# The first three levels of the next head's inverse move into the PE groups of this head's last three

## What is computed

```python
kk = jnp.einsum('bhcid,bhcjd->bhcij', kc, kc)
tri = jnp.where(strict, bc[..., :, None] * kk * decay, 0.0) + jnp.eye(CHUNK, dtype=f32)
rhs = jnp.concatenate([vc * bc[..., None], kc * (bc * jnp.exp(G))[..., None]], axis=-1)
sol = lax.linalg.triangular_solve(tri, rhs, left_side=True, lower=True, unit_diagonal=True)
u, w = sol[..., :GDN_DV], sol[..., GDN_DV:]
...
def step(S, inp):
    v_new = u_c - w_c @ S
    o = qd_c @ S + qk_c @ v_new
    S = cd_c * S + kd_c.T @ v_new
    return S, o
o = rmsnorm(o, o_norm_g) * silu(gate)
```

## Time and profile before

| | before |
|---|---|
| median of the runs | 1357.52 us |
| the profiled execution's own time | 1352.9 us |
| its span, first to last instruction | 1351.1 us |
| PE busy | 98% of the span |
| VectorE busy | 58% |
| ScalarE busy | 44% |
| granted PE clock, mean | 0.998 of full speed |

### The profile page before, as it was taken

How to read it: one execution, slowest core, us unless ns; L and a number is a source line. 1 busy time by engine, 2 the same in 40 slices (tenths; PEclk the granted TensorE clock), 3 DMA queues, 4 the chain that set the end, 5 groups by cost and what they waited for, 6 DMA issues and landing times.

```text
span 1351.1 us, 21851 instructions
## 1 busy us (share of the span) xinstructions
PE 1322.4 (98%) x8305; PEld 1061.6 (79%) x8305; DVE 779.4 (58%) x1160; ACT 600.5 (44%) x940; POOL 0.2 (0%) x4
## 2 busy tenths in 40 slices
PE   7899999999999999999999999999999999999998
PEld 5677777776888888888887877778888888888886
DVE  6787888887464344343455677776543433434555
ACT  5565556655353133231345667754431422313342
POOL 0000000000000000000000000000000000000000
PEclk9999999999999999999999999999999999999999
DMA  4332222321333323333333322224333333333323
GB/s 157 95 79 41 70 77 62 78 62 48 114 105 99 104 83 105 93 102 100 85 102 126 109 63 63 63 79 156 94 109 94 94 96 91 109 93 93 93 82 105
DMA packets 42342, 124.02 MB, mean 92 GB/s; under 512 B 3952, under 2 KB 12720, under 8 KB 41776
## 3 DMA queue, kind: packets, MB, share of 16 engines
q1 hardware_dynamic: 33472, 116.95, 28.8%
q10 hardware_dynamic: 8816, 6.33, 2.6%
HBM read 119.04 MB, written 4.23 MB: 91 GB/s over the span
## 4 chain that ended last, share of the span: by engine, by line
PE 88%; DVE 5%; ACT 4%; issue 2%; DMA 1%; ACTq 0%; DVEq 0%; SPq 0%
PE acc L333 26%; PE acc L335 25%; PE acc L334 25%; DVE wl L309 1%; DVE work L1716 1%; PE ps L485 1%; ACT wh L302 1%; PE ps L455 1%; PE ps L705 1%; PE ps L428 1%; DMA work<-rows 1%; PE ps L678 1%; PE ps L333 1%; PE ps L335 0%; PE ps L334 0%
## 5 line engine op out<-in xcount | busy, mean ns | idle before, releaser
L333 PE MATMUL acc<-xh,wh 128*128 128x512 f32 x1008 | 414.4, 411 | 11.5 <-DVE xl L1899 8.2
L335 PE MATMUL acc<-xh,wl 128*128 128x512 f32 x1008 | 394.8, 392 | 0.0
L334 PE MATMUL acc<-xl,wh 128*128 128x512 f32 x1008 | 394.3, 391 | 0.0
L302 ACT ACTIVATE wh<-raw 128x1024 fp32r<-128x1024 f32 x207 | 216.9, 1050 | 183.5 <-DMA raw<-in_weights 165.6
L309 DVE TENSOR_TENSOR wl<-raw,wh 128x1024 fp32r<-128x1024 f32 x207 | 253.0, 1222 | 67.5 <-ACT wh L302 64.6
L333 PE MATMUL acc<-yh,wh 128*128 128x512 f32 x608 | 238.1, 392 | 0.0
L334 PE MATMUL acc<-yl,wh 128*128 128x512 f32 x608 | 236.6, 389 | 0.0
L335 PE MATMUL acc<-yh,wl 128*128 128x512 f32 x608 | 236.6, 389 | 0.0
L333 PEld LDWEIGHTS acc<-xh,wh 128*128 128x128 f32 x1008 | 190.0, 188 | 52.6 <-DVE wl L309 10.1
L335 PEld LDWEIGHTS acc<-xh,wl 128*128 128x128 f32 x1008 | 189.9, 188 | 41.0
L334 PEld LDWEIGHTS acc<-xl,wh 128*128 128x128 f32 x1008 | 190.4, 189 | 36.0 <-issue 2.6
(11 more groups left out here) (252 smaller groups left out, 1105.8 us busy)
## 6 DMA issues: line engine op xcount, KB each, us to landing
raw<-in_weights SPq DMA_DIRECT2D x208, 512.0 KB, 3.5
work<-rows ACTq DMA_DIRECT2D x16, 256.0 KB, 7.1
h<-in_xT SPq DMA_DIRECT2D x4, 512.0 KB, 6.0
proj<-work ACTq DMA_DIRECT2D x2, 1024.0 KB, 5.3
work<-proj SPq DMA_DIRECT2D x2, 1024.0 KB, 6.7
outT<-h SPq DMA_DIRECT2D x8, 256.0 KB, 2.4
cst<-in_cst SPq DMA_DIRECT2D x1, 512.0 KB, 3.1
work<-in_pT SPq DMA_DIRECT2D x1, 512.0 KB, 4.6
```

The costliest lines, as they stand in the source:

```text
L302: nc.scalar.activation(slot(u)[0][:], raw[u.const % 2][:], ACT.Copy).then_inc(hi_done, 1)
L333: nc.tensor.matmul(dst[:], hi, mh[:, k, :], start=(n == 0), stop=False)
L334: nc.tensor.matmul(dst[:], hi, ml[:, k, :], start=False, stop=False)
L335: mm = nc.tensor.matmul(dst[:], lo, mh[:, k, :], start=False, stop=(n == KT - 1))
```

## The change

Two heads are now in work at once. The inverse's levels 1 to 3 of head i ("early") are computed in the same PE groups as levels 4 to 6 of head i-1 ("late"), so that a head has 6 groups (`x_group`, `tx_group`, r = 0, 1, 2). In a group the late matmuls come first, then 16 early ones on 32x32 tiles into another bank or another part of the bank. The level-6 matmuls are now 8 on tiles of 64 rows by 32 columns. Head 0's early levels stand alone, in six groups, and the last head's late levels too.

The early inverse lives as packed 32-wide blocks (128x128 instead of 128x512), so VectorE's masks, additions and transposes shrink to 64 or 128 columns, and after level 3 the blocks are put back on the diagonal of `TT` by four small transposes. `k`, `Lt`, `Ti`, the decay table, exp(G) and k by token have two buffers, and GpSimd copies `k` and `Lt` from the early buffer to the late one, 128x512 each, once per head. Because levels are ahead, the unit order changes to k of head i+1, then q, v and gate of head i; PE begins with five units, and period 7 has three. ScalarE copies k by token out of PSUM first (`act_ksq`) and scales it later (`token_k`). The ones matmul of the norm becomes two matmuls on a high and a low part (`osh` by ScalarE, `osl` by VectorE). The qk step moves from os(0) to v(3). On PE periods 2 to 6 are a loop and period 7 is written out; on VectorE and ScalarE all periods are written out, with no loop.

The diff, cut to its core:

```diff
+        kcs, qc, vc, sq, dbeta = [W(0), W(14)], W(1), W(2), W(3), W(4)
+        T64, xrstd = W(5)[:, 0:C * HD], W(6)
+        Tis = [W(5)[:, 2 * P:3 * P], W(5)[:, 3 * P:]]
...
-        TT0, xrstd = W(5), W(6)
-        Ti, TT, Xs, kb, kd, vb = W(16), W(17), W(18), W(19), W(20), W(21)
...
+        Tts, TT0, Xe = [W(16)[:, 0:P], W(16)[:, P:2 * P]], W(16)[:, 2 * P:3 * P], W(16)[:, 3 * P:3 * P + HD]
+        TT, Xl, kb, kd, vb = W(17), W(18)[:, 0:C * HD], W(19), W(20), W(21)
...
+        def kk_bank(j):
+            return ps[4 if isinstance(j, int) and j == 1 else 0]
...
+        def pe_norm(pe, j):
+            pe.wait_ge(ones_d, 1)
+            pe.wait_ge(s_d, j * 3 + 3)
+            pe.wait_ge(osh_d, j + 1)
+            nc.tensor.matmul(ps[4][:], ones_r, osh, start=True, stop=False)
+            pe.wait_ge(osl_d, j + 1)
+            nc.tensor.matmul(ps[4][:], ones_r, osl, start=False, stop=True).then_inc(oss_d, 1)
...
+        def x_group(pe, i, r, late, early):
+            b, e = i - 1, i
+            if late:
+                if r == 0:
+                    pe.wait_ge(te_d, b * 4 + 4)
+                    if not isinstance(i, int) or b > 0:
+                        pe.wait_ge(l_kept, b)
+                else:
+                    pe.wait_ge(tl_d, b * 2 + r)
+                if r == 2:
+                    pe.wait_ge(t64_d, b + 1)
+            if early:
+                pe.wait_ge(te_d, e * 4 + r + 1)
+                pe.wait_ge(ktok_d, 2 if isinstance(e, int) and e == 0 and r > 0 else e + 1)
+            small_tile(pe, i)
+            if late:
+                Lt, Ti = Lts[0], Tis[0]
+                for c in range(C):
+                    if r == 0:
+                        for lo in range(0, P, 32):
+                            q = slice(lo, lo + 32)
+                            last = nc.tensor.matmul(blk32(ps[0], c)[q], ch(Lt, c)[q, q], blk32(Ti, c)[q],
+                                                    start=True, stop=True)
+                    elif r == 1:
+                        for lo in (0, HD):
+                            one, two = slice(lo, lo + 32), slice(lo + 32, lo + HD)
+                            last = nc.tensor.matmul(blk32(ps[0], c)[two], ch(Lt, c)[one, two], blk32(Ti, c)[one],
+                                                    start=True, stop=True)
+                    else:
+                        for lo in (HD, HD + 32):
+                            q = slice(lo, lo + 32)
+                            last = nc.tensor.matmul(ps[0][q, c * HD:(c + 1) * HD], ch(Lt, c)[0:HD, q],
+                                                    T64[0:HD, c * HD:(c + 1) * HD], start=True, stop=True)
+            if early:
+                Lt, Ti = Lts[now(e)], Tis[now(e)]
+                for c in range(C):
+                    for lo in range(0, P, 32):
+                        q = slice(lo, lo + 32)
+                        last = nc.tensor.matmul(blk32(ps[2], c)[q], ch(Lt, c)[q, q], blk32(Ti, c)[q],
+                                                start=True, stop=True)
+            last.then_inc(xg_d, 1)
...
+            if early:
+                Tt = Tts[now(e)]
+                for c in range(C):
+                    to = slice(c * 16, (c + 1) * 16)
+                    for lo in range(0, P, 32):
+                        q = slice(lo, lo + 32)
+                        last = nc.tensor.matmul(ps[1][:, 2 * P:][q, to], blk32(TT0 if r == 0 else Tt, c)[q], Xe[q, to],
+                                                start=True, stop=True)
+            last.then_inc(txg_d, 1)
...
-                pe.wait_ge(tt_d, i * 6)
+                pe.wait_ge(ttl_d, i * 3)
+                if early:
+                    pe.wait_ge(te_d, i * 4 + 4)
+                pe.wait_ge(kbkd_d, i)
                 for c in range(1, C):
...
-        FILL = [0, 2, 2, 0, 2, 2, 2, 2, 2, 2, 2, 2, 2, 1, 1, 1, 1, 1, 1, 1, 1, 1, 1]
-        FIRST_FILL = [6, 2, 2, 0, 1, 2, 1, 2, 1, 2, 1, 2, 1, 1, 1, 1, 1, 1, 1, 1, 1, 1, 0]
-        assert sum(FILL) == sum(FIRST_FILL) == 4 * KT
...
+        def pe_first_steps(pe):
+            def x(r):
+                return lambda: x_group(pe, 0, r, False, True)
+            def tx(r):
+                def step():
+                    tx_group(pe, 0, r, False, True)
+                    if r == 0:
+                        pe_ktr(pe, 1)
+                        pe_kk(pe, 1)
+                return step
+            return [x(0), tx(0), x(1), tx(1), x(2), tx(2)]
...
+        FILL = [3, 3, 0, 3, 3, 3, 3, 2, 1, 2, 1, 2, 1, 2, 1, 2]
+        FIRST_FILL = [2, 1, 1, 1, 1, 1, 1] + [2, 2, 0, 1, 2, 1, 2, 1, 2, 1, 2, 1, 2, 1, 2, 2]
+        SHORT_FILL = [2, 2, 0, 2, 2, 2, 2, 2, 1, 2, 1, 1, 1, 1, 1, 2]
+        LAST_FILL = [1, 2, 0, 1, 2, 1, 2, 1, 1, 1, 2, 1, 2, 1, 2, 5, 10]
         OUT_AHEAD = ((5,), (5,), (5,), (5,), (), (), (), (2,))
-        LAST_FILL = [1, 1, 0, 1, 1, 1, 1, 1, 1, 2, 2, 1, 1, 1, 1, 1, 1, 1, 1, 1, 1, 3, 10]
-        assert sum(LAST_FILL) == 5 * (KT - 1)
+        assert sum(FILL) == sum(FIRST_FILL) == 4 * KT and sum(SHORT_FILL) == 3 * KT and sum(LAST_FILL) == 5 * (KT - 1)
...
+            gates = dict(zip((8, 12, 17, 21), pe_gate_steps(pe)))
+            for n in range(5 * KT):
+                if n in gates:
+                    gates[n]()
+                if n == KT:
+                    pe.wait_ge(s_keep, 16)
+                    pe.wait_ge(x_sq, KT - 1)
+                    nc.tensor.matmul(ps[0][:], ones, accb, start=True, stop=True).then_inc(rs_mm, 1)
+                if n == KK_FIRST_AT:
+                    pe_ktr(pe, 0)
+                    pe_kk(pe, 0)
+                next(todo)
+            for _ in todo:
+                pass
+            pe_qk(pe, 0)
+        KK_FIRST_AT = 32
...
+        def pe_period(pe, i, fill, steps, todo):
+            for step, n in zip(steps, fill):
+                step()
+                for _ in range(n):
                     next(todo)
...
+        @block.gpsimd
+        def _(pool):
+            for j in range(1, H):
+                pool.wait_ge(k_silu, j + 1)
+                pool.wait_ge(qk_d, j)
+                nc.gpsimd.tensor_copy(kcs[0], kcs[1]).then_inc(k_kept, 1)
+                pool.wait_ge(lt_d, j + 1)
+                pool.wait_ge(xg_d, 3 * j + 3)
+                nc.gpsimd.tensor_copy(Lts[0], Lts[1]).then_inc(l_kept, 1)
...
+        def act_start(act):
+            s1, s2, s3 = act_gate_steps(act)
+            act.wait_ge(g_pe, 1)
+            split_hi(act, Unit(3))
+            s1()
+            act_tap(act, 1, 0)
+            s2()
+            split_hi(act, Unit(4))
+            s3()
+            act_tap(act, 1, 1)
+            act_silu(act, 1, 0)
+            act.wait_ge(g_dma, 16)
+            act_rows(act, 0)
+            act_silu(act, 1, 1)
+            act_tap(act, 0, 0)
+            split_hi(act, Unit(5))
+            act_silu(act, 0, 0)
+            act.preload_act_table_set(LN_EXP)
+            act_ksq(act, 0)
+            act_decay(act, 0)
+            act_eg(act, 0)
+            act.wait_ge(a_d, 1)
+            act.wait_ge(eg_d, 1)
+            act_rows(act, 1)
+            act_tap(act, 2, 0)
+            act.wait_ge(s_keep, 16)
+            nc.scalar.activation(ones_r, ones, ACT.Copy).then_inc(ones_d, 1)
...
+            def token_k():
+                act.wait_ge(ktok_d, i)
+                if b > 0:
+                    act.wait_ge(w_d, b)
+                    act.wait_ge(su_d, b * 3)
+                for c in range(C):
+                    if c < C - 1:
+                        nc.scalar.activation(ch(kd, c), ch(ktoks[b % 2], c), ACT.Copy, scale=tc(3, c, b))
+                    if c > 0:
+                        ins = nc.scalar.activation(ch(kb, c), ch(ktoks[b % 2], c), ACT.Copy, scale=tc(2, c, b))
+                ins.then_inc(kbkd_d, 1)
...
+                src = diagonal(Lt, q).rearrange("p c (g two) -> p c g two", two=2)[:, :, :, 1]
+                mask = cst[q, 0:16].unsqueeze(1).broadcast_to([32, C, 16])
+                ins = nc.vector.tensor_tensor(odd, src, mask, ALU.mult)
+            ins.then_inc(id_d, 1)
...
+        def dve_masks(dve, i, r, late, early):
+            dve.wait_ge(xg_d, 3 * i + r + 1)
+            if late and r == 0:
+                if i > 1:
+                    dve.wait_ge(txg_d, 3 * i)
+                ins = nc.vector.tensor_tensor(packed(Xl, 4), chunk_halves(ps[0][:, 0:P], 4, 0), level_mask(4), ALU.mult)
+            elif late and r == 1:
+                dve.wait_ge(txg_d, 3 * i + 1)
+                ins = nc.vector.tensor_scalar(Xl[:, 0:P], ps[0][:, 0:P], -1.0, None, ALU.mult)
+            if early:
+                ins = nc.vector.tensor_tensor(packed(Xe, r + 1), chunk_halves(ps[2][:, 0:P], r + 1, 0),
+                                              level_mask(r + 1), ALU.mult)
+            ins.then_inc(xsg_d, 1)
```

More of the change, by code:

```diff
@@ L579, in pe_out_steps, with pe_start @@
             yield
[L581 to L586 removed]
+        def pe_start(pe):
             def x_gate(k):
```

(15 more changed lines are left out.)

1022 lines of the change are left out of this document (537 added, 485 removed).

## The result

| | before | after |
|---|---|---|
| median of the runs | 1356.82 us (4 runs, 1354.58 to 1359.9) | 1338.34 us (4 runs, 1336.68 to 1340.73) |
| ratio, 95% interval | | 0.9864 (0.9838 to 0.9889) |
| profiled execution | 1352.9 us | 1340.73 us |
| its span | 1351.1 us | 1338.9 us |
| mean granted PE clock | 0.998 | 0.992 |

The change is 18.5 us faster by the medians, where 12.0 were forecast. Profile against profile it is 12.2 us, the sum almost to the digit. That agreement is an accident, as the experiments show: the profiled execution of before was among its shortest, that of the changed kernel the longest of its four.

What follows compares the result with a forecast made beforehand. The prediction took PE, busy 1322.4 of 1351.1 us, to bound the kernel. Groups 12.1, norm 3.2 and period 8's 1.3 gained, less 4.6 lost in the start, gave 12.0 us less: 1345.5 us, range 1339 to 1354.

Steps and rivals of the forecast that it cites:

- Level groups, 12.1 us: PE's level groups: joining late and early parts takes 48.2 us against 60.3, 12.1 gained, 5.84 per period with both parts.
- fixed part of 0.28 per group: PE's level groups: of 0.57 us per group, 0.28 is fixed, 0.09 of it ahead and the rest behind.
- 0.10 for a change of shape: Joint r = 2 groups: changing from 64x32 to 32x32 tiles inside the group adds 0.10 us, making 1.20.
- Rival B: Joint groups: the second part does not run beside the first; gain only 1.7 us, time 1355.8; chance 0.09.
- Norm, 3.2 us: Norm on PE: float32 matmul of 0.86 us becomes two passes of 0.46; eight times 0.40, 3.2 us gained.
- The loop's other engines at nothing: Loop: VectorE, ScalarE and GpSimd come in time, so PE's waits for them are costed at nothing.
- rivals C: Loop: PE waits about 1 us per period for VectorE or ScalarE, six times; time 1351.5 us; chance 0.16.
- D: Loop: GpSimd's copy of k holds VectorE and delays tx group 0; slower, 1364.7 us at 4.5 us held; chance 0.06.
- only fewer or cheaper PE pieces gain time: Loop: with PE busy 38.09 of 38.10 us, nothing else gains time, and only if no other engine comes late.
- Period 8, 1.3 us: Period 8: two unit steps fill PE's 1.1 us wait for level 6's copy, and some 0.2 of small ones go.
- The start, 4.6 us lost: Start: PE's waits and low-clock losses (1.2 us per stretch) rise from 6.3 to 10.9 us, 4.6 lost.
- so the median becomes 1357.5 - 12.0: Whole kernel: the 12.0 us gain, taken from the median of before, 4.6 above the profiled execution, gives 1345.5 us.

Runs made afterwards that it cites:

- the groups apart: Changed kernel with, in periods 2 to 7, one unit step between each group's late and early part: 1344.87 us, 0.9925 of before.
- the interleaved ones: Changed kernel with late and early parts of the r = 2 groups interleaved chunk by chunk, seven shape changes instead of one: 1348.16 us, 0.9943 of before.
- the test: Kernel before with one unit step of each head moved from behind `w` to ahead of it: 1354.21 us against 1355.56, ratio 0.9986.
- before again: Kernel before, unedited, run once more for its trace: 1354.34 us.
- the changed kernel again: Changed kernel, unedited, measured again against the kernel before: 1337.35 us against 1355.56, ratio 0.9867.
- the filler test: Changed kernel with 29 unused 128x512 matmuls (9, 15 and 5) put into three PE waits of the start: 1333.45 us, 0.9837 of before.
- the filler test in before: Kernel before with unused matmuls, 12 ahead of head 1's first group and 6 ahead of unit 5's first step: 1357.2 us against 1356.11, ratio 1.0011.
- the second refilled start: Changed kernel with v0 taken earlier, period 1's unit steps spread anew, and k2's take and two units' splits moved: 1331.63 us, 0.9832 of before.

## Why the prediction was wrong, point by point

- **Level groups, 12.1 us:** right, and a little small. 5.71 instead of 5.84 a head makes 13.0. The fixed part of 0.28 per group (0.27 by the groups apart) and 0.10 for a change of shape (0.12 by the interleaved ones) both hold. Rival B is out.
- **Norm, 3.2 us:** right, 3.4 by the spacings, 3.0 to 3.9 by undoing it.
- **The loop's other engines at nothing:** right for the changed kernel. PE waits for none of them in the loop, and rivals C and D did not occur.
- **A wait of before that had no term:** in each of the six heads of the loop, `w` waited 0.28 us of path time for level 6's write, 1.7 us in all (1.6 by the period of the test, 1.35 by its medians). The prediction says that in the loop "only fewer or cheaper PE pieces gain time", from PE busy for 38.09 of 38.10 us; but busy there counts matmuls to their modelled ends, and a wait shorter than that overlap is not seen.
- **Period 8, 1.3 us:** too small by more than half. PE in this period, before again and then the changed kernel again:

```profile
319.49 0.45 PE L455 MATMUL ps<-work 32*32 32x32 f32 x32
321.29 0.65 PE L485 MATMUL ps<-work 32*32 32x64 f32 x32 [0.46 <-DVE work L1399]
323.79 0.45 PE L455 MATMUL ps<-work 32*32 32x32 f32 x32 [0.51 <-DVE work L1409]
...
339.37 0.65 PE L494 MATMUL ps<-work 64*64 64x64 f32 x8 [1.12 <-ACT work L932]
...
386.48 1.02 PE L648 MATMUL ps<-work,kept 128*128 128x512 f32 x2
```

```profile
308.97 0.45 PE L519 MATMUL ps<-work 32*32 32x32 f32 x32
...
368.59 1.02 PE L796 MATMUL ps<-work,kept 128*128 128x512 f32 x2
```

From the first group to the same later matmul (L648, now L796), with 72 unit steps between in both, it was 66.99 us and is 59.62: 7.4 less. Six groups fewer make 3.7 of that and two norms 0.8. The other 2.9 are waits that are gone. Before has four of them here, 0.46, 0.51, 0.30 and 1.12; the prediction counted the last and put the rest at "some 0.2 of small ones". Together they are 2.4; the other 0.5 stand in no list of waits.

- **The start, 4.6 us lost:** about 3 by what is left. With 13.0 + 3.4 + 1.7 + 2.9 = 21.0 gained elsewhere, the usual 17.5 us (1355.6 less 1338.1, the median of the changed kernel's eight runs; the spans of before again and the changed kernel again, 1352.5 and 1335.0, differ by the same 17.5) leaves 3.5 lost. Some 0.3 of it lies behind the last rows above, where the rest of the execution takes 966.4 us and took 966.0. The waits themselves were right to 0.1 us each. The low clock was mis-sized, and on both sides: in the changed kernel 3.9 us go to it by the filler test, where 2.4 stood in the sum, and in the profiled execution it was up to 10; before has 1.7 in its best execution, where 1.2 stood in the sum, and more in its usual one.
- **The steps that failed.** The usual difference is 5.5 us more than the 12.0 forecast. Most of that are gains the sum had too small: the wait of `w`, put at nothing by "only fewer or cheaper PE pieces gain time" (1.7); "1.1 gained, and some 0.2 of small ones" in period 8, where 2.9 were (1.6); the groups (0.9) and the norm (0.2). The start gives the rest, 1.1 with what lies behind it. From 1345.5 to the usual 1338.1 are 7.4 us; the further 1.9 come from "so the median becomes 1357.5 - 12.0": 1357.5 was the median of three runs, and 50 runs gave 1355.6.
- **Why profile against profile looked right.** The 12.2 us between the two profiled executions set the shortest start of before against a changed kernel with 20 us at the low clock. By this pair the start lost 8.8 us, not 4.6, and that covered the gains that were missed. The 4.6 us between the profiled execution of before and the median belonged to that execution and that median. How the start's loss divides between the load, the issue gaps and the clock of before stays open: the filler test in before, which was to tell, only moved its low clock.

## What to carry to other kernels

A sum made against one profiled execution inherits that execution's luck: where runs scatter by more than the effect of a term, take two or three traces of before, or at least ask for the granted clock by windows, before the offset to the median is carried over. The waits of before that a change may remove deserve the same care as its large terms: list them all, by period. For a line that must follow another engine's write closely, ask the trace for that line alone: the list of waits hides gaps shorter than the modelled overlap of matmuls, and six that cost 0.28 us each were there. A wait of a few microseconds in the dense PE stream here cost its length and then 1.7 us or more of slow matmuls behind it. Filling such waits with useless matmuls gained 3.9 us in the changed kernel and nothing in the kernel before, where the clock fell behind other gaps.

## What the hardware showed that was not expected

- 29 useless matmuls of 128x512 in three waits made the kernel 3.9 us faster and its runs closer (range 2.2 us instead of 6.1).
- PE showed gaps of up to 2.6 us on "issue" in code met for the first time, in every trace but that of the groups apart, where the list of waits has none. The clock fell behind some (2.5 us at 105 us in the second refilled start, 0.74) and not behind others (1.7 us in the kernel with filled waits, 1.00). What sets them no run shows.
- A change between 64x32 and 32x32 tiles costs 0.12 us. Within a group of one shape (r = 1) the late and early records mix in the trace, and the x group with both parts takes 0.83, less than that of r = 0 with 0.88.
- A GpSimd copy of 128x512 takes 0.61 us, and VectorE's passes of two SBUF inputs beside it take 0.4 longer. The Trainium skill (SBUF — State Buffer, SBUF: two separate sides) says that such passes exclude each other for a whole instruction; the rows agree in kind, since each of the two got longer beside the other. They do not show a wait for the copy's full length (0.4 of 0.61), nor which of the two held the pass back and for how long.
